# Overflow of an expert computed in strips of 32 slots in four column groups, with the second strip in a branch of its own; two orders near it changed

## The reference, cut to what matters

```python
logits = (xt @ router_w + router_b).astype(jnp.float32)
top_v, top_i = lax.top_k(logits, TOP_K)          # 4 of 32, for 256 tokens
gates = jax.nn.softmax(top_v, axis=-1)
...
def expert_block(args):
    idx, e = args
    xb = xpad[idx]
    gu = xb @ w_gate_up[e] + b_gate_up[e]        # 1024 -> 2048
    x_glu = jnp.minimum(gu[:, ::2], SWIGLU_LIMIT)
    x_lin = jnp.clip(gu[:, 1::2], -SWIGLU_LIMIT, SWIGLU_LIMIT)
    act = x_glu * jax.nn.sigmoid(SWIGLU_ALPHA * x_glu) * (x_lin + 1.0)
    return act @ w_down[e] + b_down[e]           # 1024 -> 1024
```

## Time and profile before

| | |
|---|---|
| median of 3 executions | 2475.5 us (2474.22 to 2480.19) |
| the profiled execution | 2479.43 us |
| its span, first to last instruction | 2477.6 us |
| TensorE busy | 2252.4 us, 91% |
| VectorE busy | 857.1 us, 35% |
| ScalarE busy | 412.9 us, 17% |
| mean rate of all transfers | 265 GB/s |
| mean granted TensorE clock | 0.957 of full speed |

### The profile page before, as it was taken

The page is one execution under the profiler, slowest core; times in us unless marked ns, Lnnn a source line. Parts: engine busy times, 40 slices in busy tenths (PEclk is TensorE's granted clock), DMA queues, the critical chain, the costliest instruction groups (busy, mean ns, idle before and its releaser), DMA issues. The chain is left out here.

```text
span 2477.6 us, 25057 instructions
## 1 busy us (share of the span) xinstructions
PE 2252.4 (91%) x9764; PEld 1301.2 (53%) x9764; DVE 857.1 (35%) x1745; ACT 412.9 (17%) x893; POOL 109.0 (4%) x79
## 2 busy tenths in 40 slices
PE   7998999988899888888879999998799999989998
PEld 4655443333334333333337688666558755547873
DVE  4664222111212111111137436554557202343201
ACT  1222111111111011111022322112321001222100
POOL 1000000000000000000000000001100000000000
PEclk8998999999999999999989999998899999989999
DMA  9767498999999999999977721764157443323441
GB/s 359 256 242 306 168 369 316 412 412 413 412 337 412 413 412 412 412 412 413 413 277 286 272 85 52 267 231 147 68 187 258 166 153 137 136 102 128 153 161 43
DMA packets 212510, 657.19 MB, mean 265 GB/s; under 512 B 8591, under 2 KB 13303, under 8 KB 195669
## 3 DMA queue, kind: packets, MB, share of 16 engines
q1 hardware_dynamic: 208528, 649.53, 68.8%
q0 software_dynamic: 1808, 3.65, 0.4%
q10 hardware_dynamic: 2004, 1.67, 0.2%
HBM read 653.77 MB, written 1.05 MB: 264 GB/s over the span
## 5 line engine op out<-in xcount | busy, mean ns | idle before, releaser
L1619 PE MATMUL ps<-w,XE 128*64 128x512 f32 x1280 | 351.4, 614 | 46.9 <-DMA w<-in_w_gate_up 29.4
L815 PE MATMUL ps<-HF,w 128*128 128x256 f32 x1408 | 311.6, 384 | 1.8 <-DVE CF L3055 1.8
L815 PEld LDWEIGHTS ps<-HF,w 128*128 128x128 f32 x1408 | 271.7, 193 | 42.2 <-issue 4.5
L1619 PEld LDWEIGHTS ps<-w,XE 128*64 128x64 f32 x1280 | 113.4, 141 | 261.9 <-issue 250.0
L1649 DVE TENSOR_TENSOR T<-ps,BB 128x512 f32<-128x512 f32 x64 | 44.3, 692 | 592.0 <-PE ps L1619 592.0
L1690 PE MATMUL ps<-w,AT 128*64 128x512 f32 x640 | 177.6, 610 | 20.5 <-DMA w<-in_w_down 14.3
L815 PE MATMUL ps<-HT,w 128*128 128x256 f32 x768 | 178.0, 390 | 6.4 <-DVE dqk L2405 3.7
L815 PEld LDWEIGHTS ps<-HT,w 128*128 128x128 f32 x768 | 148.2, 196 | 29.9 <-issue 8.7
L637 DVE SCALAR_TENSOR_TENSOR AUX<-w,CS,AUX 128x512 f32<-128x512 f32 x210 | 157.9, 752 | 7.5
L833 PE MATMUL ps<-w,AF 128*128 128x512 f32 x352 | 151.6, 593 | 1.8 <-DVE AF L3077 1.8
L833 PE MATMUL ps<-w,HT 128*128 128x512 f32 (+1 forms) x352 | 148.2, 576 | 0.3 <-DVE S L1463 0.3
(11 more groups left out here) (595 smaller groups left out, 2624.8 us busy)
## 6 DMA issues: line engine op xcount, KB each, us to landing
w<-in_w_gate_up SPq DMA_DIRECT2D x80, 2048.0 KB, 22.1
w<-in_w_down SPq DMA_DIRECT2D x40, 2048.0 KB, 22.4
w<-in_ada_w SPq DMA_DIRECT2D x24, 2048.0 KB, 8.1
w<-in_ffn_w_in SPq DMA_DIRECT2D x20, 2048.0 KB, 8.1
w<-in_w_in SPq DMA_DIRECT2D x17, 2048.0 KB, 9.8
tables<-in_w_gate_up SPq DMA_DIRECT2D x16, 2048.0 KB, 23.6
GR<-in_w_gate_up SPq DMA_DIRECT2D x16, 2048.0 KB, 24.1
AUX<-in_w_gate_up SPq DMA_DIRECT2D x16, 2048.0 KB, 23.6
```

What stands on the lines that cost most here:

```text
L815: ins = e.matmul(out_, w[:, k, c:c + n], HT[:, k, :], start=k == 0, stop=k == kc - 1, skip_group_check=True)
L1619: ins = e.matmul(b[j * n:j * n + n, :], FM.XE[:, side(x), 4 * kh + k, j * n:j * n + n], ring.tile(512, 1024, "gu", ex_, h, kh, x[0])[:, k, ...
```

## The change

The overflow of an expert is no longer computed as 64 slots in two column groups of 512 outputs each, but in strips of 32 slots in four column groups of 256 outputs each. Strip 0 (slots 64 to 95) runs where the expert has over 64 tokens. Strip 1 (slots 96 to 127) stands in an `If` within that branch, for over 96. Each TensorE instruction of gate/up now reads every second pair of elements of the weight row (`every_other`), two of each four fp32 values. A second flag per expert is made and read, on TensorE alone. The half of the down bank that strip 1 would fill is written with zeros by one matmul. The scatter becomes 16 matmuls of 32 rows.

`more_gather_dve` runs for every expert and no longer in a branch. The transposes of the gates for the bias of the down product (`GT`) move from `down_bias_pe` up to the router, and their copy out of PSUM moves to ScalarE. In `start_pe` the rows of tile 2 and the sum of tile 1 stand ahead of or behind `turn_pe` in another order. In the router, `ada_part_dve(15)` and `ada_rows_sum_pe(15)` stand earlier.

```diff
-        f.flag, f.mxc = sb("flag", [128, 33], I32, c=ph), sb("mxc", [128, 34], c=ph)
-        f.ACCM, f.GT = sb("ACCM", [128, 2, D], c=ph), sb("GT", [32, 256], c=ph)
+        f.flag, f.mxc = sb("flag", [128, 65], I32, c=ph), sb("mxc", [128, 66], c=ph)
+        f.ACCM, f.GT = sb("ACCM", [128, 2, D], c=ph), f.RW[0:32, :, :].rearrange("p k n -> p (k n)")
...
+        ada_rows_pe(e, 2, CSB)
+        ada_rows_sum_pe(e, 1)
         e.wait_ge(*at("first", "xn"))
         turn_pe(e, "first", lambda t, k: m.first.XN[:, t, cols(k)], 8)
-        ada_rows_sum_pe(e, 1)
-        for n in (2, 3):
-            ada_rows_pe(e, n, CSB)
-            ada_rows_sum_pe(e, n)
+        ada_rows_sum_pe(e, 2)
+        ada_rows_pe(e, 3, CSB)
+        ada_rows_sum_pe(e, 3)
...
-        for t in range(2):
-            ins = e.transpose(b[:, cols(t)], FM.PG[:, 1, t, :], ident)
+        for s in range(2):
+            for t in range(2):
+                ins = e.transpose(b[:, 256 * s + 128 * t:256 * s + 128 * t + 128], weighted(s)[:, t, :], ident)
...
+    def every_other(row, g):
+
+        return row.rearrange("p (q n j a) -> p q j n a", q=2, j=2, a=2)[:, g // 2, g % 2]
...
-        for g in range(2):
-            e.matmul(b[64 * g:64 * g + 64, :], ones[row, 0:64], FM.BR[row, 1024 * h + 512 * g:1024 * h + 512 * g + 512], start=True,
-                     stop=False, skip_group_check=True)
...
+        for g in range(4):
+            e.matmul(b[strip(g)], ones[row, 0:32], every_other(FM.BR[row, 1024 * h:1024 * h + 1024], g), start=True, stop=False,
+                     skip_group_check=True)
         for kh in range(2):
             w = ring.tile(512, 1024, "gu", ex_, h, kh, x[0])
             for k in range(4):
-                for g in range(2):
-                    ins = e.matmul(b[64 * g:64 * g + 64, :], XM(j)[:, 4 * kh + k, :], w[:, k, 512 * g:512 * g + 512], start=False,
+                for g in range(4):
+                    ins = e.matmul(b[strip(g)], XM(j, s)[:, 4 * kh + k, :], every_other(w[:, k, :], g), start=False,
                                    stop=kh == 1 and k == 3, skip_group_check=True)
...
+            b = bank2.take(e, x, "down", "more", j)
+            e.matmul(b[:, 256:512], ident, C("SU", 0, 1).broadcast_to([128, 256]), start=True, stop=True, skip_group_check=True)
...
-                for g in range(2):
-                    ins = e.matmul(b[64 * g:64 * g + 64, :], FM.XE[:, 2, 4 * d + 2 * j + k % 2, 64 * (k // 2):64 * (k // 2) + 64],
-                                   w[:, k, 512 * g:512 * g + 512], start=d == 0 and k == 0, stop=d == 1 and k == 3,
-                                   skip_group_check=True)
...
+                for g in range(4):
+                    ins = e.matmul(b[strip(g)], AT(j, s)[:, 4 * d + k, :], w[:, k, 256 * g:256 * g + 256],
+                                   start=d == 0 and k == 0, stop=d == 1 and k == 3, skip_group_check=True)
...
+        for s in range(2):
+            v = bank(x, "turned", "more", j).rearrange("p (h s g n) -> p s h g n", h=2, s=2, g=4)[:, s]
+            e.activation(AT(j, s).rearrange("p (h g) n -> p h g n", h=2), v, ACT.Copy).then_inc(*wide["act"](x, "at", "more", j))
...
             with e.If(over[j] == 1):
-                part(e, x, j, *args)
+                part(e, x, j, 0, *args)
+                n1 = extra.n
+                with e.If(over[2 + j] == 1):
+                    part(e, x, j, 1, *args)
+                with e.Else():
+                    passed(e, extra, n1)
+                if last is not None:
+                    last(e, x, j)
...
     def down_bias_pe(e):
-        b = bank2.take(e, "GT")
-        for t in range(2):
-            ins = e.transpose(b[0:32, cols(t)], FM.G[:, t, :], ident)
-        ins.then_inc(*pe("GT"))
         e.wait_ge(*at("GT", "out"))
...
-        e.wait_ge(*at("GT"))
-        e.tensor_copy(FM.GT[:, :], bank("GT")[0:32, 0:256]).then_inc(*dve("GT", "out"))
-        dve.leave("bank", "GT")
```

More of the change, by code:

```diff
@@ L1818, in more_down_pe, with more_scatter_pe @@
+        ins.then_inc(*wide["pe"](x, "down", "more", j, s))
+        if s:
+            for d in range(2):
+                wide["pe"].leave("w", "down", ex_, d, x[0])
+    def more_scatter_pe(e, x, j):
         e.wait_ge(*at(x, "y", j))
+        bs = [bank2.take(e, x, "scs", j, g) for g in range(4)]
         for t in range(2):
-            for hf in range(2):
-                b, rows = bank2.take(e, x, "sc", j, t, hf), slice(64 * hf, 64 * hf + 64)
-                e.matmul(b, FM.PGT[rows, 2 + j, cols(t)], AM(j)[rows, :], start=True, stop=True,
-                         skip_group_check=True).then_inc(*wide["pe"](x, "sc", j, t, hf))
+            for s in range(2):
+                for g in range(4):
+                    ins = e.matmul(bs[g][:, 256 * t:256 * t + 256], FM.PGT[strip(g), 2 + 2 * j + s, cols(t)],
+                                   AM(j)[strip(g), 256 * s:256 * s + 256], start=s == 0, stop=s == 1, skip_group_check=True)
+        ins.then_inc(*wide["pe"](x, "scs", j))
@@ L1825, in more_down_act, with more_scatter_dve @@
+    def more_scatter_dve(e, x, j):
+        own(e, dve)
+        own(e, wide["dve"])
+        e.wait_ge(*at(x, "scs", j))
+        for g in range(4):
+            o = FM.ACCM[:, :, 256 * g:256 * g + 256]
+            e.tensor_tensor(o, o, bank(x, "scs", j, g).rearrange("p (t n) -> p t n", t=2), ADD).then_inc(*wide["dve"](x, "acc"))
+            wide["dve"].leave("bank", x, "scs", j, g)
     def more_down_act(e, x, j):
         e.wait_ge(*at(x, "turned", "more", j))
-        v = FM.XE[:, 2, :, :].rearrange("p (d i) n -> p d i n", d=2)[:, :, 2 * j:2 * j + 2, :]
@@ L1828, in more_down_act @@
-        e.activation(v, bank(x, "turned", "more", j).rearrange("p (d i n) -> p d i n", d=2, i=2), ACT.Copy).then_inc(
-            *wide["act"](x, "at", "more", j))
+        for s in range(2):
+            v = bank(x, "turned", "more", j).rearrange("p (h s g n) -> p s h g n", h=2, s=2, g=4)[:, s]
+            e.activation(AT(j, s).rearrange("p (h g) n -> p h g n", h=2), v, ACT.Copy).then_inc(*wide["act"](x, "at", "more", j))
         wide["act"].leave("bank", x, "turned", "more", j)
-        e.wait_ge(*at(x, "down", "more", j))
+        e.wait_ge(*at(x, "down", "more", j, 1))
@@ L1838, in more, with strips @@
+    def more(e, x, over, who, part, *args):
+        for j in range(2):
+            n, users = wide[who].n, [list(b.user) for b in (gu_bank, bank2)]
+            with e.If(over[j] == 1):
+                part(e, x, j, *args)
+            with e.Else():
+                passed(e, wide[who], n)
+            if who == "pe":
+                both_users(users)
+    def strips(e, x, over, part, *args, last=None):
+        extra = wide["pe"]
         for j in range(2):
@@ L1860, in pair_pe @@
         gate_up_pe(e, x, 0, 1)
-        more(e, x, over, "pe", more_gate_up_pe, 0)
+        strips(e, x, over, more_gate_up_pe, 0)
         between_pe(e, p)
@@ L1865, in pair_pe @@
         gate_up_pe(e, x, 1, 1)
-        more(e, x, over, "pe", more_gate_up_pe, 1)
+        strips(e, x, over, more_gate_up_pe, 1)
         down_pe(e, x, 0, range(3))
@@ L1870, in pair_pe @@
         down_pe(e, x, 1, range(4))
-        more(e, x, over, "pe", more_down_pe)
+        strips(e, x, over, more_down_pe, last=more_scatter_pe)
     def between_pe(e, p):
@@ L1904, in pair_dve @@
         e.wait_ge(*at(x, "pg turned"))
-        more(e, x, over, "dve", more_gather_dve)
+        own(e, wide["dve"])
+        for j in range(2):
+            more_gather_dve(e, x, j)
         if p + 1 < len(PAIRS):
@@ L2054, in moe_pe @@
         e.matmul(b[:, 64:96], ones, FM.sl[:, 1, :], start=False, stop=True, skip_group_check=True).then_inc(*pe("ranks"))
-        ada_rows_sum_pe(e, 15)
+        b = bank.take(e, "GT")
+        e.wait_ge(*at("gates"))
+        for t in range(2):
+            ins = e.transpose(b[0:32, cols(t)], FM.G[:, t, :], ident)
+        ins.then_inc(*pe("GT"))
         gu_bank.user, bank2.user = bank.user[0:4], bank.user[4:8]
@@ L2073, in moe_act @@
         bias_act(e, PAIRS[0])
+        e.wait_ge(*at("GT"))
+        e.activation(FM.GT[:, :], bank("GT")[0:32, 0:256], ACT.Copy).then_inc(*act("GT", "out"))
+        act.leave("bank", "GT")
         gather_act(e, PAIRS[0])
@@ L2097, in moe_dve @@
         e.wait_ge(sems["router_landed"], 48)
+        ada_part_dve(e, 15)
         for t in range(2):
```

117 lines of the change are left out of this document (65 added, 52 removed).

## The result

The changed kernel takes 2560.3 us (median of 4 executions, 2559.30 to 2565.65) against 2477.2 us before (4 executions, 2474.22 to 2480.19). The ratio is 1.0342, with a 95% interval of 1.0329 to 1.0355. The profiled execution took 2565.65 us, with a span of 2563.8 us. The forecast was 2456, and neither the range nor the rival for "slower" (2487) held it.

A forecast was written before the change was run, and what follows sets the result against it. TensorE was taken to set the pace until 411 us and around 700, loads elsewhere. Terms -0.9 - 2.4 - 8.45 (expert 0) - 9.35 (expert 3) + 1.5 (expert 13) = -19.6 from 2475.5 gave 2456 us, range 2447 to 2470.

The forecast's parts named there:

- the rival for "slower" (2487): Gate/up strips: the strided moving operand halves the pace, 0.427 us a round, net +11 us; chance 0.13.
- The pace of a strip: Overflow gate/up: 72 records, four at once, make 18 rounds of 0.213 us, 3.84 us plus 0.2 for the tail.
- records at 66 ns: Overflow strips: records follow only every 66 ns, 0.05 us more a round, +10.6 us, so 2466; chance 0.12.
- Down and scatter: Expert 0's overflow: down falls from 7.09 to 4.65 us, -2.45; scatter 1.9 against 1.99 us, no gain.
- What gains bring at 410 us: Mixture: TensorE's gains up to 410 us bring the loads forward equally and are kept; the 410.34 load goes out near 390.
- The start, -0.9,: Start: transposes replace tile 2's sum, which waited 0.91 us for a copy; no new wait on a load, -0.9 us.
- `GT`, -2.4,: Before the bias matmuls: two transposes and a 2.01 us wait for the copy move into the router's waits, -2.4 us.
- Expert 13, +1.5,: Pair 6, both strips needed: gate/up unchanged, down +0.7, transposes and two inner branches +0.8, in all +1.5 us.
- one more `Else` with its drain: Expert 0's gate/up strip on TensorE: the added branch priced like the 0.31 us in front of L1926.
- In pairs without overflow TensorE's queue reads them ahead of its matmuls: Pairs without overflow: the two more flag reads cost nothing; +1.3 us was counted only at the start of pair 1.
- elsewhere the loads set it: Mixture: TensorE sets the pace until 411 us and around 700; otherwise loads do, TensorE idling 28 of 280 and 56 of 496 us.
- the signs that I had named for a wrong forecast: 7 us strips; idle before L1805 ending in VectorE; a non-overflow pair's TensorE awaiting flags with DMA share under 1.

The follow-up runs named there:

- with one strip: The changed kernel without its inner branch, so slots 96 to 127 of expert 13 are never computed and bodies shrink: 2456.4 us, ratio 0.9931.
- strips in pairs 0 and 1: The changed kernel with strips only in pairs 0 and 1, the parts of the kernel before in the other 14: 2465.1 us, ratio 0.9946.
- the moved steps alone: The kernel before with only the order in start_pe, GT in the router, and the two tile 15 steps earlier: 2471.4 us, ratio 0.9987.
- the two kernels with strips: The changed kernel with strips only in pairs 0, 1 and 6 (2472.4 us), and only in pairs 0 and 1 (2465.1 us).
- long bodies and no strip: The kernel before with never-taken matmuls making its TensorE branch bodies as long as the changed kernel's: 2578.6 us, ratio 1.0423.
- at a DMA share of 0.34: The changed kernel with weight loads of experts 16 to 31 cut to 0.5 MB of each 2 MB tile: 2491.0 us, one execution.

## Why the prediction was wrong, step by step

- **The pace of a strip** was nearly right: 0.213 us a round forecast, 0.219 measured, and 4.41 us for the 72 records where 3.84 and 0.2 were forecast. The 64 records of L1805 last 3.83 us and not "about 3.5". Both rivals about it, records at 66 ns (55 measured) and the strided operand at half pace, were wrong.
- **Down and scatter** were right for expert 0: 3.66 us for the 64 records of L1835 where 3.41 and a tail were forecast, and 2.01 for the scatter. For expert 3 the same 64 records took 5.35 us, behind a jump of 6.27 us at 386.3, in a window with a granted clock of 0.72; with one strip, where that jump is short, they took 3.66.
- **What gains bring at 410 us.** The load of the earlier trace rows at 410.34, by the timeline of SyncE in three kernels: the changed one, the one with one strip, and the one with strips in pairs 0 and 1:

```profile
400.40 1.34 SPq L195 DMA_DIRECT2D GR<-in_w_gate_up  x1
```

```profile
389.03 0.46 SPq L195 DMA_DIRECT2D GR<-in_w_gate_up  x1
```

```profile
399.89 0.46 SPq L195 DMA_DIRECT2D GR<-in_w_gate_up  x1
```

With one strip it comes 21.3 us earlier, and the kernel is 17 us faster. With strips in pairs 0 and 1 it comes 10.5 earlier and the kernel is 13 us faster, and with the moved steps alone 4.4 and 3.2. So the chain "pace up to 410 us, kept behind it" holds within some 4 us. In the changed kernel the load comes 9.9 us earlier, half of the forecast 20. The 11 us between the second and the third kernel are jumps in pairs 0 and 1, past expert 1's and expert 2's bodies and past the inner ones: all branches from 233 to 412 us are 8.2 us with one strip and 18.5 with both, and one of them took 6.09 us.
- **The start, -0.9,** failed: "the row shows no wait on a load where it stands now, so I take no new one". One came, of 2.67 us in the changed kernel, and pair 0 began at 237.63 where it had begun at 237.48. `GT`, -2.4, was right for the wait, which is gone with the moved steps alone; in the changed kernel a wait of 2.25 us for the `Else` of expert 1 took its place.
- **Expert 13, +1.5,** was mis-sized: 6 to 7 by the two kernels with strips, of which the jump above explains at least 2.61.
- **The step that failed** is the one that priced a branch: "one more `Else` with its drain", 0.3 us, and with it "In pairs without overflow TensorE's queue reads them ahead of its matmuls", said of the flags and the only thing that the sum said of TensorE in those pairs. It counted instructions that run. The 342 matmuls a pair that do not run were priced at nothing, in 13 of 16 pairs. They made 22.2 us of branches a pair where 2.0 stood before, of which TensorE's queued matmuls hide 8.1. The 14 that are left, less the 7.8 that TensorE idled before, and 0.9 for the clock are the 7.2 us a pair.
- **The cover** was there, but thin: TensorE was idle for 7.8 us a pair before, and the jumps then made it idle for 14.2. "elsewhere the loads set it" was true up to that bound, and the prediction did not state the bound.
- **The clock** is a consequence: 0.90 and not 0.96 in those pairs, 0.9 of the 7.2 us. It falls with long bodies and no strip (0.941 over the whole run, 0.954 to 0.961 before), and it falls behind idle times, those of 2.16, 6.51 and 8.95 us above.

Of the signs for the forecast, the down tiles of pair 0 went out at 260.81 and not near 259, the idle time in front of L1992 was 2.25 us and not under 0.5, and the window from 300 to 390 had a DMA share of 0.90 and not near 1. Of the signs that I had named for a wrong forecast, the last came true in its second half: TensorE stood in pairs without overflow while the DMA share was under 1, but for code and not for flags.

## What to carry to other kernels

Price a branch by what it jumps past. In these kernels code that is not run cost TensorE's queue nothing at 18 fp32 matmuls a body; from 27 to 72 a growing share of the jumps was slow, and from 96 on every jump timed was a stall of about 6 us, whatever the distance. Keep rare bodies short, put one jump around several of them, and put other matmuls between two jumps. Count such jumps in the common case, not in the one that the body is for, and compare their sum with the cover there is: the idle time per stage that the loads leave, and what the matmuls already queued hide, here some 3 us a place.

## What the runs showed of the hardware

- A jump of TensorE's queue cost 0.21 us, about 3.5 or 6.1 us beside full loads, by whether its target had been brought, was on its way, or was fetched only after the jump had begun; 96 and 640 matmuls cost the same. It ended 1.4 to 1.5 us behind the packet. In the changed kernel single jumps took up to 7.7 us.
- The packets of the instruction queue are 16.4 KB, some 64 fp32 matmuls, and are held up by weight loads: at a DMA share of 0.34, 20 of 28 slow jumps took 2.8 to 3.8 us and none 5.4 to 6.2, where at 0.96 20 of 54 took 5.4 to 6.2.
- Fp32 matmuls whose moving operand is two of each four values ran nearly as fast as contiguous ones: 3.83 to 3.88 us for 64 records in four column groups of 256, against 3.66.
